# Moving the expert dots 16 slots ahead, the gelu to step 2, the attention to six slots a head, and the dots' shared operand to PSUM

## What is computed

```python
q = (xt @ w_q).reshape(T, PEER_HEADS, 2, PEER_HALF)
s_half = jnp.einsum('thcd,hcnd->thcn', q, keys)          # 8 heads, 2 x 128 keys
sv, si = lax.top_k(s_half, PEER_TOPK)                    # top 16 of each half
cand = sv[:, :, 0, :, None] + sv[:, :, 1, None, :]       # 256 sums a head
cv, ci = lax.top_k(cand.reshape(...), PEER_TOPK)         # top 16 of those
...
u = jnp.take(w_u, ec, axis=0)                            # 128 rows of w_u a token
h = jnp.einsum('cd,ced->ce', xc, u)
a = jax.nn.gelu(h) * gc
y = jnp.einsum('ce,ced->cd', a, jnp.take(w_v, ec, axis=0))
```

## Time and profile before

| what | value |
|---|---|
| median of 3 runs | 3777.69 us (3771.69 to 3777.8) |
| profiled execution, own time | 3777.35 us |
| its span | 3775.5 us |
| DMA in the span | 1240.83 MB, mean 329 GB/s |
| DVE / ACT / POOL busy | 2217.4 / 1600.3 / 2360.9 us |
| first gather starts / last gather starts | 530.8 / 3754.5 us |

### The profile page before, as it was taken

How to read it: one execution, slowest core, us unless ns; L and a number is a source line. 1 busy time by engine, 2 the same in 40 slices (tenths; PEclk the granted TensorE clock), 3 DMA queues, 4 the chain that set the end, 5 groups by cost and what they waited for, 6 DMA issues and landing times.

```text
span 3775.5 us, 40818 instructions
## 1 busy us (share of the span) xinstructions
PE 2722.5 (72%) x14008; PEld 2179.7 (58%) x14008; DVE 2217.4 (59%) x5004; ACT 1600.3 (42%) x1836; POOL 2360.9 (63%) x2075
## 2 busy tenths in 40 slices
PE   6999966578788676577887775677986665565545
PEld 3456745456675565466775664566765554444444
DVE  5143067458765676477765685578655774467533
ACT  1121014345454444354554454454544453344434
POOL 4000028766677767766677787756776777677775
PEclk9999987578799886698898895787998885655656
DMA  4235459998999999998999999989999999999997
GB/s 167 86 106 173 151 171 353 356 348 314 345 409 409 392 363 356 362 342 330 358 409 404 375 379 350 359 319 331 399 409 391 381 343 351 349 357 345 353 359 291
DMA packets 350432, 1240.83 MB, mean 329 GB/s; under 512 B 38480, under 2 KB 46160, under 8 KB 349712
## 3 DMA queue, kind: packets, MB, share of 16 engines
q0 software_dynamic: 294912, 1073.87, 75.2%
q1 hardware_dynamic: 34096, 117.94, 8.5%
q10 hardware_dynamic: 21216, 46.40, 3.4%
HBM read 1222.33 MB, written 15.73 MB: 328 GB/s over the span
## 4 chain that ended last, share of the span: by engine, by line
PE 29%; POOL 24%; issue 13%; another core or an unknown queue 10%; DMA 8%; ACT 7%; DVE 6%; DVEq 3%; SPq 0%; ACTq 0%
POOL rows L319 12%; POOL rows L310 11%; PE acc L600 9%; DMA rows<-in_peer_v,ids_peer 7%; ACT av L1099 5%; PE fA L523 3%; PE m L567 2%; PE fA L483 2%; PE m L371 2%; PE m L499 2%; PE acc L589 1%; DVE rows L872 1%; PE fB L341 1%; PE fB L535 1%
## 5 line engine op out<-in xcount | busy, mean ns | idle before, releaser
L600 PE MATMUL acc<-ident,av 128*128 128x128 f32 x8192 | 1394.9, 331 | 904.3 <-ACT av L1099 587.2
L600 PEld LDWEIGHTS acc<-ident,av 128*128 128x128 f32 x8192 | 1176.8, 172 | 1137.8 <-ACT av L1099 692.5
L1099 ACT ACTIVATE av<-rows,coef 128x1024 f32<-128x1024 f32 x1024 | 1161.4, 1145 | 1479.6 <-DMA rows<-in_peer_v,ids_peer 563.5
L310 POOL DMA_INDIRECT rows<-in_peer_u,ids_peer x1024 | 1137.2, 1111 | 807.3 <-DVE ids_peer L852 339.5
L872 DVE CUSTOM_DVE_ANT_0 rows<-rows,hh 128x1024 f32<-128x1024 f32 x1024 | 1235.7, 1222 | 651.3 <-DMA rows<-in_peer_u,ids_peer 573.8
L319 POOL DMA_INDIRECT rows<-in_peer_v,ids_peer x1024 | 1175.6, 1148 | 444.0 <-issue 292.4
L567 PE MATMUL m<-hT_g,wring 128*128 128x256 f32 x1024 | 249.2, 400 | 1.1 <-ACT hT_g L1061 1.1
L523 PE MATMUL fA<-hT_g,wring 128*128 128x256 f32 x1024 | 241.7, 392 | 0.9 <-issue 0.9
L567 PEld LDWEIGHTS m<-hT_g,wring 128*128 128x128 f32 x1024 | 203.4, 204 | 29.7 <-ACT hT_g L1061 1.5
L523 PEld LDWEIGHTS fA<-hT_g,wring 128*128 128x128 f32 x1024 | 199.1, 199 | 29.0 <-issue 2.4
L768 DVE COPY S<-fB 128x1024 f32<-128x1024 f32 x64 | 78.2, 1222 | 151.9 <-PE fB L341 69.1
(11 more groups left out here) (153 smaller groups left out, 2173.5 us busy)
## 6 DMA issues: line engine op xcount, KB each, us to landing
wring<-in_wstream SPq DMA_DIRECT2D x192, 512.0 KB
ln<-in_dft_seq ACTq DMA_DIRECT2D x32, 512.0 KB, 3.4
rows<-in_peer_u,ids_peer POOLq DMA_INDIRECT x1024
rows<-in_peer_v,ids_peer POOLq DMA_INDIRECT x1024
hT_g<-in_x SPq DMA_DIRECT2D x8, 512.0 KB, 3.6
hres_spill<-KT ACTq DMA_DIRECT2D x8, 512.0 KB, 2.7
hT_spill<-rows ACTq DMA_DIRECT2D x1, 4096.0 KB
wring<-in_wstream SPq DMA_DIRECT2D x16, 256.0 KB
```

The source lines that it names most:

```text
L310: pool.indirect_dma_start(u_rows[:, ring(g, i, NU), :], None, peer_u, bass.IndirectOffsetOnAxis(ap=ids_peer[:, t, s:s + 1], axis=0)).then_ ...
L600: last = mm(acc[:, tok(k)], av[:, i % NAV, tok(k)], ident[:, :], is_transpose=True, start=i % SLOTS == 0 and k % 4 == 0, stop=i % SLOTS == ...
L1099: s.activation(av[:, i % NAV, :], v_rows[:, ring(g, i, NV), :], ACT.Copy, scale=coef[:, b, i % BATCH:i % BATCH + 1]).then_inc(scaled, 1)
```

## The change

Three things change. The dots run 16 slots ahead of the scales in place of 12, the gelu stands at step 2 of 8 in place of 4 (the coefficients stay at step 5), and LEAD falls from 64 to 40. The attention takes 6 steps a head in place of 4; every later part of the front starts later, and the second tile's retrieval has 16 steps a head in place of 12. The h1 of the dots is copied once a tile into a PSUM tensor, h1_ps. For that fB is given up: in group 0's front h1_ps still serves as fB, in later groups the transposes of the probabilities go into fA, where the scores are too, and the scores of a head then wait for the copy of the head before. The other users of fB take m0 and m1, which are now one tensor mB.

```diff
-AHEAD = 12
-LEAD = 64
+AHEAD = 16
+LEAD = 40
...
-A0, A_PERIOD = 0, 4
-M0, M_PERIOD = 72, 6
-O0 = 120
-L0 = 136
-K0, K_PERIOD = 148, 4
+A0, A_PERIOD = 0, 6
+M0, M_PERIOD = 99, 6
+O0 = 147
+L0 = 163
+K0, K_PERIOD = 175, 4
 
 T0, T_PERIOD = K0 + 2 * K_PERIOD + 1, 2 * K_PERIOD
-R0, R_PERIOD = 27, 12
+R0, R_PERIOD = 46, 16
...
-        fA, fB = ps("fA", 1024), ps("fB", 1024)
-        m0, m1 = ps("m0", 512), ps("m1", 512)
-        banks = (fA[:, 0:512], fA[:, 512:1024], fB[:, 0:512], fB[:, 512:1024])
+        fA, h1_ps, mB = ps("fA", 1024), ps("h1_ps", D), ps("mB", 1024)
+        m0, m1 = mB[:, 0:512], mB[:, 512:1024]
+        banks = (fA[:, 0:512], fA[:, 512:1024], h1_ps[:, 0:512], h1_ps[:, 512:1024])
+        fbanks = (fA[:, 0:512], fA[:, 512:1024], m0, m1)
+
+        def turned(g):
+            return h1_ps if isinstance(g, int) and g == 0 else fA
...
+                        if u > 0 and turned(g) is fA:
+                            pe.wait_ge(probsT_sb, g * TILES * H + u)
...
-                            last = tr(fB[:, tok(k)], probs[:, tok(k)])
+                            last = tr(turned(g)[:, tok(k)], probs[:, tok(k)])
...
-                        v.tensor_copy(probsT, fB[:, :]).then_inc(probsT_sb, 1)
+                        v.tensor_copy(probsT, turned(g)[:, :]).then_inc(probsT_sb, 1)
...
+                if i % SLOTS == 0:
+                    dve.drain()
+                    v.tensor_copy(h1_ps[:, :], h1_peer[:, t, :])
+                    dve.drain()
                 row = u_rows[:, ring(g, i, NU), :]
                 b = i // BATCH % 2
-                v.tensor_tensor_reduce(out=row, in0=row, in1=h1_peer[:, t, :], scale=1.0, scalar=0.0, op0=ALU.mult,
+                v.tensor_tensor_reduce(out=row, in0=row, in1=h1_ps[:, :], scale=1.0, scalar=0.0, op0=ALU.mult,
                                        op1=ALU.add, accum_out=dots[:, b, i % BATCH:i % BATCH + 1]).then_inc(u_free, 1)
...
-                if m % BATCH == 4 and has_slot(g, m + LEAD + BATCH, last):
+                if m % BATCH == 2 and has_slot(g, m + LEAD + BATCH, last):
```

More of the change, by code:

```diff
@@ L511, in front @@
                     a = M0 + M_PERIOD * dc
-                    gb, yb = banks[dc % 2], banks[2 + dc % 2]
+                    gb, yb = fbanks[dc % 2], fbanks[2 + dc % 2]
                     for j in range(2):
@@ L545, in front @@
                             for half in range(2):
-                                last = mm(banks[2 * t + half], mT[:, k, tok(t)], w[:, half * 512:(half + 1) * 512],
+                                last = mm(fbanks[2 * t + half], mT[:, k, tok(t)], w[:, half * 512:(half + 1) * 512],
                                           start=k == 0, stop=k == KD - 1)
@@ L553, in front @@
                         for k in range(KD):
-                            last = tr((fA, fB)[t][:, tok(k)], h1_front[:, t, tok(k)])
+                            last = tr((fA, mB)[t][:, tok(k)], h1_front[:, t, tok(k)])
                         last.then_inc(h1T_ps, 1)
@@ L783, in front @@
                         v.tensor_tensor(prod[:, :, :].rearrange("p a b -> p (a b)"),
-                                        sg[:, :, :].rearrange("p a b -> p (a b)"), banks[2 + dc % 2], ALU.mult)
+                                        sg[:, :, :].rearrange("p a b -> p (a b)"), fbanks[2 + dc % 2], ALU.mult)
                         dve.drain()
@@ L792, in front @@
                             dve.wait_ge(hres_in, 16 * (g + 1))
-                        v.tensor_tensor(h1_front[:, t, :], h1_front[:, t, :], (fA, fB)[t][:, :], ALU.add)
+                        v.tensor_tensor(h1_front[:, t, :], h1_front[:, t, :], (fA, mB)[t][:, :], ALU.add)
                         dve.drain()
@@ L1046, in front @@
                         for j in range(2):
-                            last = s.activation(sg[:, j, :], banks[dc % 2][:, j * GROUP:(j + 1) * GROUP], ACT.Sigmoid,
+                            last = s.activation(sg[:, j, :], fbanks[dc % 2][:, j * GROUP:(j + 1) * GROUP], ACT.Sigmoid,
                                                 bias=bg[:, j, dc:dc + 1])
@@ L1060, in front @@
                         act.wait_ge(h1T_ps, g * TILES + t + 1)
-                        s.activation(hT_g[:, :, tok(t)], (fA, fB)[t][:, :].rearrange("p (k t) -> p k t", k=KD),
+                        s.activation(hT_g[:, :, tok(t)], (fA, mB)[t][:, :].rearrange("p (k t) -> p k t", k=KD),
                                      ACT.Copy).then_inc(h1T_sb, 1)
```

## The result

| | median, us | runs | lowest to highest |
|---|---|---|---|
| before | 3777.74 | 4 | 3771.69 to 3780.14 |
| changed | 3919.17 | 4 | 3914.17 to 3928.48 |

The ratio is 1.0377, with a 95% interval of 1.0358 to 1.0396: **slower by 141 us**. The forecast was 3562 us, its range ended at 3740. Direction and size were wrong.

A forecast was written before the change was run, and what follows sets the result against it. POOL's gather cost and its waits were taken as the bound, with DMA binding in three stretches. From 3777 us, -170 - 40 - 40 + 5 + 10 + 10 + 10 = -215 gave 3562 us, range 3440 to 3740.

The forecast's parts named there:

- the third rival: PE's late av signals to ACT set the pace, so half of 170 and both 40s go: 3727 us, chance 0.13.
- Dots in PSUM, -170 us: POOL's gathers beside DVE's dots shorten once h1 is read from PSUM, partly hidden by DMA: -170 us.
- the four fifths: Dots' assumed part of POOL's 388 us gather excess over the median: 310 us, before deducting what is hidden.
- Gelu and 16 ahead, -40 us: A stopped ACT stops DVE's coefficients later, returning some of POOL's 317.6 us of waits: -40 us.
- Six slots a head, -40 us: Attention stages cost 77 us more than slots alone; thinner spreading of heads returns half: -40 us.
- the hand-over (c), +10 us: Row numbers reach POOL closer to their gathers; blocking costs some 130 us if POOL always runs ahead, taken as +10.
- Prologue (a), +10 us: Group 0's front, before gathers: five heads left after the dft's work lack PE cover, 2 us each: +10, from 0 to 20.
- fA shared (b), +10 us: In later groups the scores wait for the previous head's copy, 45 times, mostly already done: +10 us.
- The rival of 3845 us: Single score buffer: each head's copy and late signal delay the next scores, 6.5 us a head, 45 heads; chance 0.11.
- Copy, +5 us: DVE's copies into h1_ps, 8 times 1.22 us, 10 us at most, half in slack: +5 us.
- Table loads (d): Twelve more table loads of 1.28 us on ACT, covered by its wait for v rows: 0, or 15 us without cover.
- DMA's limit, 3440 us: Rival: gathers speed up all the way to DMA's limit, 372 us less the 35 of costs: 3440 us, chance 0.08.

The follow-up runs named there:

- The run that would tell the two apart: Changed kernel plus one 128x1 memset on POOL ahead of each gather: 3513.9 us, 0.9872 of the kernel before, on a chip without late PE signals.

## Why the prediction was wrong, step by step

- **The step that failed is in the third rival:** "The change does not touch this". The late signals were seen (427 us, 10.08 us in the timeline) and taken as a fixed tax of the kernel, worth half of the gains at worst. They are no fixed tax: ACT's waits without a releaser are 829.2 and 883.6 us in the changed kernel, and 452.8 with h1 back in SBUF and all else as changed. The step that was priced at -170 us is the one that brings them. It was priced by what POOL gains alone, and the range had no case in which a faster gather makes PE's signals worse; its only case on the slow side was 5.3 us of lateness at every head, in place of more stops at the slots.
- **Dots in PSUM, -170 us.** The premise was right: the gathers fell by 376.5 us of 388, more than the four fifths I gave them. The page "SBUF — State Buffer" of the Trainium skill, section "Who interferes with whom", infers for tensor_tensor that two SBUF inputs do not stall the making of descriptors; for this dot, which has two as well, the runs disagree, 1140 ns a gather with both operands in SBUF and 943 with one in PSUM, all else the same. What that is worth was right on the punctual chip (-121 us) and wrong in sign on the late one: 3919.17 against 3833.1, some +85 us.
- **Gelu and 16 ahead, -40 us.** Alone 1.004 on a punctual chip, a loss of 6 to 22 us by its interval. The coefficients' idle time did fall, from 140.1 to 90.9 us, and to 6 on the punctual chip, but no time came back with it. The prediction had named the reason, that gather_v waits for ACT's scale all the same, and took -40 anyway.
- **Six slots a head, -40 us, and the hand-over (c), +10 us.** Together with LEAD 1.0196 / 1.004: a loss of 1.6%. The attention's slots did get shorter (240 us for 152 gathers, 3.16 us a slot, with h1 in SBUF on the late chip, row below, where they took 3.4), but the waits for row numbers took more than that back. They were priced at 10 where the bound said 130: 474.8 - 355.9 = 119 us in 16 waits. POOL's lead of 6 steps was called rare; in fact it waits at 16 of the 19 places.

```profile
810.00:1050.00 240.00, 170.81 (x1024) 143.04 (x1023) 164.29 (x351) 130.75 (x140) 170.27 (x152) 0.82 0.95 359
```

- **Prologue (a), +10 us.** The first gather starts at 547.3 us where it was 530.8: +16.5, within the 0 to 20.
- **fA shared (b), +10 us:** no difference on the punctual chip (3630.21 against 3630.42), 20.3 us of waits on the late one. The rival of 3845 us is refuted as a mechanism: a head cost no 5 us.
- **Copy, +5 us:** 9.8 us of DVE, as worked out. **Table loads (d):** the gelu's went from 73 to 78, at 1283 ns; no run here prices them.
- **DMA's limit, 3440 us.** On a punctual chip the changed kernel runs against it nearly everywhere (395 to 398 GB/s); what keeps it 70 us above 3440 no run shows. Taking away the waits for row numbers (LEAD 32) brought 7.

Of the 141 us the runs thus place about 55 in the table, LEAD, AHEAD and the gelu's step (0.0147 x 3777.74) and about 85 in the dots' operand (1.0377 / 1.0147 - 1 = 2.3%). The interval of the 1.0147 makes each of the two uncertain by 18 us.

What stays open. Why PE's completions are late on some chips and not on others, under equal DMA load, no run here shows; the same chip number was met in both kinds, so it need not be the chip. That the *pace* of the gathers makes the signals later, and not DVE's reads of PSUM together with a full DMA, is not shown; the run that would tell the two apart did not meet a late chip. LEAD 32 was not run on a late chip either. And a version with the dots in PSUM and the old table, which the ratios suggest for a punctual chip, needs fB's place in PSUM and was not tried.

## What to carry to other kernels

When a profile has large waits that nothing in it explains, ask what condition they come with before taking them for a constant. Here they came only with a busy DMA, and a change that left DMA busy for just as long still doubled them. So price a change's effect on such waits, too, and look at the lateness of the signals themselves, not only at how long the condition holds. When an engine's work shrinks by some hundred us, close its account afterwards (work, issue gaps, waits by releaser): the row that grew names the new bound. A table of numbers that spreads a front more thinly has to be paid at its end; here the hand-over was the price. LEAD 32 removed those waits, but where DMA was the bound only 7 of their 170 us came back as time.

## What the runs showed of the hardware

- The same kernel takes 3562 us on some chips and 3778 us on others, 6% apart, with no wait without a releaser on the first and 427 us of waits for late PE signals on the second. Two kernels can change order between them: 0.9852 and 1.0377.
- An indirect gather of 128 rows of 4 KB costs POOL 0.94 us, and a mean of 1.14 beside dots with two SBUF operands (up to 1.995). With one operand in PSUM the mean is 0.943 to 0.951.
- On the chips of 3778 us, PE's signals come late only while DMA is busy: 0.67 us behind in the mean at a DMA share of 0.8 or more, 0.01 below it; 1.46 and 0.02 with the dots' operand in PSUM. On the chips of 3562 us they are 0.01 behind at any share.
- A drain of POOL behind a gather costs about 4.0 us (4083.1 us in 1024 gaps).
